# A chunked RWKV-7 mixer: 128x128 block-diagonal matrices kept as two 64x64 blocks, each product issued as two on opposite quarters of TensorE

## What is computed

```python
def rwkv7_scan(r, w, k, v, a, bvec):
    decay = jnp.exp(-jnp.exp(w))
    def step(state, inp):
        r_t, d_t, k_t, v_t, a_t, b_t = inp
        sa = jnp.einsum('bhvk,bhk->bhv', state, a_t)
        state = (state * d_t[:, :, None, :] + sa[..., None] * b_t[:, :, None, :]
                 + v_t[..., None] * k_t[:, :, None, :])
        return state, jnp.einsum('bhvk,bhk->bhv', state, r_t)
    ...
# in rwkv7_mixer, with kk normalised per head:
y = rwkv7_scan(rh, heads(w), kh, vh, -kk, kk * ah)
```

## Time and profile before

| | |
|---|---|
| median of 3 runs | 3529.41 us |
| the profiled execution | 3524.7 us, its span 3522.9 us |
| PE busy | 3341.1 us (95%) |
| DVE busy | 1490.8 us (42%) |
| ACT busy | 1082.6 us (31%) |
| POOL busy | 395.9 us (11%) |
| matmul records | 16568 |

### The profile page before, as it was taken

The page is one execution under the profiler, slowest core; times in us unless marked ns, Lnnn a source line. Parts: engine busy times, 40 slices in busy tenths (PEclk is TensorE's granted clock), DMA queues, the critical chain, the costliest instruction groups (busy, mean ns, idle before and its releaser), DMA issues. The chain is left out here.

```text
span 3522.9 us, 38396 instructions
## 1 busy us (share of the span) xinstructions
PE 3341.1 (95%) x16568; PEld 2582.1 (73%) x16568; DVE 1490.8 (42%) x2056; ACT 1082.6 (31%) x1619; POOL 395.9 (11%) x386
## 2 busy tenths in 40 slices
PE   6999999889899999999999989999998999999999
PEld 2466666666758888888877766788886888888887
DVE  6256624665444111113346442556543433333333
ACT  4243324334233111112135553233323322222211
POOL 1022202343212000000012000111211100000000
PEclk9999999999999999999999999899998999999999
DMA  5111110000042111112122010000003111110211
GB/s 234 41 60 61 72 39 24 13 13 24 1 153 75 48 48 48 48 36 91 46 72 83 36 37 18 8 1 1 1 1 150 54 48 48 48 48 30 96 44 71
DMA packets 35257, 182.33 MB, mean 52 GB/s; under 512 B 4261, under 2 KB 4261, under 8 KB 21648
## 3 DMA queue, kind: packets, MB, share of 16 engines
q1 hardware_dynamic: 22176, 133.18, 10.6%
q0 software_dynamic: 12912, 46.69, 3.4%
HBM read 161.89 MB, written 17.96 MB: 51 GB/s over the span
## 5 line engine op out<-in xcount | busy, mean ns | idle before, releaser
L537 PE MATMUL ps<-r,r 128*128 128x512 f32 x2656 | 1056.7, 398 | 14.4 <-DVE r L2022 13.2
L538 PE MATMUL ps<-r,r 128*128 128x512 f32 x2656 | 1048.0, 395 | 0.0
L539 PE MATMUL ps<-r,r 128*128 128x512 f32 x2656 | 1047.9, 395 | 0.0
L537 PEld LDWEIGHTS ps<-r,r 128*128 128x128 f32 x2656 | 501.4, 189 | 142.1 <-issue 20.7
L538 PEld LDWEIGHTS ps<-r,r 128*128 128x128 f32 x2656 | 501.7, 189 | 117.2 <-issue 3.0
L539 PEld LDWEIGHTS ps<-r,r 128*128 128x128 f32 x2656 | 501.4, 189 | 115.7
L1407 ACT ACTIVATE ar<-ps 128x512 f32<-128x512 f32 (+3 forms) x330 | 170.1, 541 | 628.1 <-PE ps L1214 119.5
L1369 ACT ACTIVATE r<-ar 128x1024 fp32r<-128x1024 f32 (+1 forms) x170 | 174.4, 1032 | 550.6 <-PE ps L539 510.6
L2015 DVE TENSOR_TENSOR r<-ar,r 128x1024 fp32r<-128x1024 f32 (+1 forms) x170 | 203.8, 1199 | 324.1 <-ACT r L1369 324.0
L527 PE MATMUL ps<-ar 128*128 128x128 f32 (+5 forms) x1844 | 278.0, 314 | 6.4 <-ACT ar L1407 3.3
L527 PEld LDWEIGHTS ps<-ar 128*128 128x128 f32 (+2 forms) x1844 | 218.9, 174 | 57.1 <-issue 31.8
(11 more groups left out here) (286 smaller groups left out, 3561.4 us busy)
## 6 DMA issues: line engine op xcount, KB each, us to landing
ar<-in_w_mod SPq DMA_DIRECT2D x24, 1024.0 KB, 4.8
ar<-in_w_gu SPq DMA_DIRECT2D x22, 1024.0 KB, 4.8
ar<-in_w_up SPq DMA_DIRECT2D x22, 1024.0 KB, 4.8
ar<-in_w_in SPq DMA_DIRECT2D x19, 1024.0 KB, 4.8
ar<-in_w_dn SPq DMA_DIRECT2D x32, 512.0 KB, 3.4
x<-ar POOLq DMA_DIRECT2D x48, 256.0 KB, 2.3
ar<-x POOLq DMA_DIRECT2D x24, 512.0 KB, 7.0
ar<-in_xT POOLq DMA_DIRECT2D x16, 512.0 KB, 13.7
```

Of the source, the lines that this page charges most:

```text
L537: M.matmul(o, whk, hi[k][:, a:a + n], start=k == 0, stop=False)
L538: M.matmul(o, whk, lo_[k][:, a:a + n], start=False, stop=False)
L539: ins = M.matmul(o, wlk, hi[k][:, a:a + n], start=False, stop=k == nk - 1)
```

## The change

The two diagonal blocks of a 128x128 matrix are kept one above the other: block 0 in partitions 0 to 63, block 1 in partitions 64 to 127, both in the same 64 columns. Four matrices now take 256 columns instead of 512. Each of the 4 matmuls of an `outer`, a `quad`, `pp` or `uw` becomes two of 64x64, one for each block h: it reads the rows of block h and writes the partitions of block h. In a `quad`, `pp` and `uw` the two lie on opposite quarters of the array (rows and output partitions both 0-63, or both 64-127). In an `outer` both read the same 64 rows (the head's channels) and write different halves of the partitions.

DVE, ACT and POOL work on 128x256 where they worked on 128x512. `rb` and `rk` are still needed as full 128x128 matrices (for `ru` and `ry`): `spread` writes their blocks to their places, as two instructions of 64x256 each instead of one of 128x512, and POOL sets the rest of the four buffers to zero once, ahead of the first mask. The masks shrink to ten of 64 columns.

```diff
+    rmask = r8.tile(10 * 64)
...
+    HALF = (slice(0, 64), slice(64, 128))
...
-    temps = [halves[j] + [r8.tile(256)] for j in range(2)]
+    temps = [[x[:, 0:256] for x in halves[j]] + [r8.tile(256)] for j in range(2)]
...
+                QUARTERS = [(n_, h) for n_ in range(4) for h in range(2)]
...
                 def outer(what, x, y):
                     key = (what, g_)
                     o = claim(key, next_of(BG), (v_evac, key))
-                    for n_ in range(4):
-                        ins = M.matmul(o[:, n_ * 128:n_ * 128 + 128], x[R, cs_(n_)], y[R, cs_(n_)], start=True, stop=True)
+                    for n_, h in QUARTERS:
+                        c = n_ * 128 + 64 * h
+                        ins = M.matmul(o[HALF[h], c64(n_)], x[R, c:c + 64], y[R, c:c + 64], start=True, stop=True)
...
                 def quad(key, x, y, *by):
-                    for n_ in range(4):
-                        ins = M.matmul(o[:, n_ * 128:n_ * 128 + 128], x[:, cs_(n_)], y[:, cs_(n_)], start=True, stop=True)
+                    for n_, h in QUARTERS:
+                        ins = M.matmul(o[HALF[h], c64(n_)], x[HALF[h], c64(n_)], y[HALF[h], c64(n_)],
+                                       start=True, stop=True)
...
-                for n_ in range(4):
-                    ins = M.matmul(o[:, n_ * 64:n_ * 64 + 64], AK[:, cs_(n_)],
-                                   Vt[:, n_ * 128 + 64 * j:n_ * 128 + 64 * j + 64], start=True, stop=True)
+                for n_, h in QUARTERS:
+                    ins = M.matmul(o[HALF[h], c64(n_)], AK[HALF[h], c64(n_)],
+                                   Vt[HALF[h], n_ * 128 + 64 * j:n_ * 128 + 64 * j + 64], start=True, stop=True)
...
+                    for Hh in HALF:
+                        M.matmul(o[Hh, n_ * 128:n_ * 128 + 64], TT_[Hh, c64(n_)],
+                                 At[Hh, n_ * 128 + 64 * j:n_ * 128 + 64 * j + 64], start=True, stop=True)
+                    for Hh in HALF:
+                        ins = M.matmul(o[Hh, n_ * 128 + 64:n_ * 128 + 128], TT_[Hh, c64(n_)],
+                                       PP[Hh, c64(n_)], start=True, stop=True)
...
-                        copy(("tnn", g_, Lv), TN, bank(("tnn", g_, Lv)))
-                    copy(("tt", g_, Lv), TT_, bank(("tt", g_, Lv)))
+                        copy(("tnn", g_, Lv), TN, bank(("tnn", g_, Lv), 256))
+                    copy(("tt", g_, Lv), TT_, bank(("tt", g_, Lv), 256))
...
-                    V.tensor_tensor(th(dst), th(bank(key)), bc4(m), ALU.mult).then_inc(*v_evac(key))
+                    V.tensor_tensor(th(dst, 64), th(bank(key, 256), 64), bc4(m, w_=64), ALU.mult).then_inc(*v_evac(key))
+
+                def spread(what, dst):
+
+                    key = (what, g_)
+                    dve.wait_ge(*product.at(key))
+                    for h, Hh in enumerate(HALF):
+                        ins = V.tensor_tensor(th(dst[Hh, :])[:, :, 64 * h:64 * h + 64], th(bank(key, 256)[Hh, :], 64),
+                                              bc4(M_IU, Hh, w_=64), ALU.mult)
+                    ins.then_inc(*v_evac(key))
...
+        for i in range(2):
+            G.memset(Arbs[i], 0.0)
+            G.memset(Arks[i], 0.0).then_inc(*p_mask(("zero", i)))
```

More of the change, by code:

```diff
@@ L418, in emit @@
     r8 = Region(H, FT)
-    rmask = r8.tile(9 * 128)
-    M_SU, M_IU, M_LO = [rmask[:, j * 128:j * 128 + 128] for j in range(3)]
-    M_UP = {1 << j: rmask[:, (3 + j) * 128:(4 + j) * 128] for j in range(6)}
+    rmask = r8.tile(10 * 64)
+    M_SU, M_IU, M_LO = [rmask[:, j * 64:j * 64 + 64] for j in range(3)]
+    M_UP = {1 << j: rmask[:, (3 + j) * 64:(4 + j) * 64] for j in range(6)}
+    M_ID = rmask[:, 576:640]
+    HALF = (slice(0, 64), slice(64, 128))
     MTs, NNs, SSs = [[r.tile(512) for r in (r8, r9)] for _ in range(3)]
@@ L1199, in group, with c64 @@
                 a0 = j * 512
-                def cs_(b_):
-                    return slice(b_ * 128, b_ * 128 + 128)
+                QUARTERS = [(n_, h) for n_ in range(4) for h in range(2)]
+                def c64(n_):
+                    return slice(n_ * 64, n_ * 64 + 64)
                 def outer(what, x, y):
@@ L2709, in group @@
                 dve.wait_ge(*v_evac.last())
-                V.tensor_tensor(th(TN), th(TN), bc4(IDN), ALU.add).then_inc(*v_step())
-                V.tensor_tensor(th(TT_), th(AT), bc4(M_UP[1]), ALU.mult).then_inc(*v_step())
+                V.tensor_tensor(th(TN, 64), th(TN, 64), bc4(M_ID, w_=64), ALU.add).then_inc(*v_step())
+                V.tensor_tensor(th(TT_, 64), th(AT, 64), bc4(M_UP[1], w_=64), ALU.mult).then_inc(*v_step())
                 dve.wait_ge(*v_step.last())
-                V.tensor_tensor(th(TT_), th(TT_), bc4(IDN), ALU.add).then_inc(*v_step(("tn", g_)))
+                V.tensor_tensor(th(TT_, 64), th(TT_, 64), bc4(M_ID, w_=64), ALU.add).then_inc(*v_step(("tn", g_)))
                 yield
                 masked("ak", AK, M_SU)
-                masked("rb", Arb[:, a0:a0 + 512], M_IU)
+                if s < 2:
+                    dve.wait_ge(*p_mask.at(("zero", s)))
+                spread("rb", Arb[:, a0:a0 + 512])
                 yield
-                masked("rk", Ark[:, a0:a0 + 512], M_IU)
+                spread("rk", Ark[:, a0:a0 + 512])
                 yield
@@ L2722, in group @@
                     dve.wait_ge(*product.at(key))
-                    V.tensor_tensor(th(Yp), th(bank(key)), bc4(IDN), ALU.add).then_inc(*v_evac(key))
+                    V.tensor_tensor(th(Yp, 64), th(bank(key, 256), 64), bc4(M_ID, w_=64), ALU.add).then_inc(*v_evac(key))
                     yield
@@ L2939, in gpsimd_program @@
                         pool.wait_ge(*product.at(("y", (s, j), Lv // 2)))
-                    G.tensor_tensor(th(AM), th(AT), bc4(M_UP[Lv]), ALU.mult).then_inc(*p_mask(("am", (s, j), Lv)))
+                    G.tensor_tensor(th(AM, 64), th(AT, 64), bc4(M_UP[Lv], w_=64),
+                                    ALU.mult).then_inc(*p_mask(("am", (s, j), Lv)))
         stage_over(pool, "rwkv", 0)
@@ L3109, in layout @@
           for L in (1, 2, 4, 8, 16, 32)]
-    m["rmask"] = np.concatenate(rm + [up[0].T] + up, 1).astype(f)
+    rm = [np.concatenate([x[:64, :64], x[64:, 64:]], 0) for x in rm + [up[0].T] + up + [i[:, None] == i[None]]]
+    m["rmask"] = np.concatenate(rm, 1).astype(f)
     m["rst64"] = np.tile((r(1024) % 64 != 0).astype(f), (128, 1))
```

## The result

The changed kernel takes 3431.32 us (median of 4 runs, 3430.62 to 3432.82) against 3529.42 us: a ratio of 0.9728, 95% interval 0.9714 to 0.9743, 98 us less. I had forecast 3472, with 3428 to 3522 as the range: the direction and the range held, the likeliest case did not. What came lies nearest my fourth rival, "the clock holds", with 16 us more than its 82. The result is only 3 us inside the lower end of the range.

What follows compares the result with a forecast made beforehand. TensorE was taken to bound the mixer, with DVE as much the bound in rounds 0 to 2. 82 us gained less 25 for the clock gave 57 off 3524.7, 3467.7, plus 4.7 for the median: 3472 us, range 3428 to 3522.

Steps and rivals of the forecast that it cites:

- fourth rival: Whole mixer: the clock does not fall, so the 82 us gain stands, 3430 to 3450 us; chance 0.18.
- price of a quad: TensorE's quads: 0.92 us before, 0.47 after if opposite quarters overlap, 0.93 as the other end if not.
- second rival: TensorE's quads: opposite quarters do not keep the pace, a quad costs up to 0.93 us, 3517 to 3535 us; chance 0.06.
- The five stretches: A full mixer step at full clock, priced in five parts: -14.0 us of 69.2 in sum.
- Rounds 0 to 2: Outer products until the first `y`, bound by DVE: narrower DVE operations give -2.5 us, 12.7 to 10.2.
- Levels 2 to 8: 18 quads save 8.1 us, new waits behind `prepare` and `finish` charged +2.0: 21.3 to 15.2 us.
- Levels 16 and 32: 12 quads save 5.4 us, waits for ACT's copies and `finish` charged +2.6: 14.1 to 11.3 us.
- What the clock gives back: Clock falls more often and returns later: 9 us of each step at half clock, 25 us lost in all.
- the case that I feared: First rival: TensorE's clock stays at 1.2 GHz through the mixer's steps, 3583 to 3691 us; chance 0.11.
- Step 0: First mixer step, without `finish` and starting at half clock: taken as -12 us.
- Steps 2 to 5: Later mixer steps, priced like step 1 at -14.0 us each; steps 1 to 5 together -70 us.
- the third: Rounds 0 to 8: DVE becomes the bound, 4 us a step of the gain lost, 3496 to 3520 us; chance 0.10.

Runs made afterwards that it cites:

- run 1: Changed kernel with both block products of each quad pair sent to block 0's quarter, DVE's `y` and ACT's level copies covering 64 partitions: 3644.28 us, ratio 1.0333.
- run 3: Changed kernel with only the outer products run block by block, four products then four, quads still in opposite pairs: 3430.89 us, ratio 0.9728.
- Run 5: Changed kernel with DVE taking the operations of `finish` ahead of those of `prepare` in each round: 3433.35 us, ratio 0.9736.
- run 7: Changed kernel with `mt`, `nn`, `ru` and `ry` of the two groups all interleaved on opposite quarters: 3419.16 us, ratio 0.9693.
- runs 6 and 10: Changed kernel with `mt` and `nn` of the two groups interleaved on opposite quarters: 3426.28 us; the same plus `ry` in pairs, `ru` not: 3399.03 us.

## Why the prediction was right in direction and 41 us too careful

The 41 us are the 25 that I took off for the clock and 16 more that the sum of the stretches missed.

- **The price of a quad: right.** 0.47 taken, 0.50 measured, and the other end, 0.93, is what one quarter costs in run 1. The rule of the Trainium skill, "TensorEngine Tiling (Array Packing)", section "Instruction Overhead" (some 60 cycles for each matmul), did not bring the second rival, and I had worked it out wrongly: 60 cycles at 2.4 GHz are 0.025 us, so 16 records would be 0.40 us (an estimate from the page's figure), below 0.47 and not near 0.93. The measured 0.031 us is 74 cycles a record, so the figure is not refuted, and by the rule splitting these products further would gain little. No run here tried that.
- **Widths: right.** DVE 0.42 and ACT 0.38 as priced; POOL's mask 0.80, in its bounds and hidden.
- **The five stretches: right in sum, by errors that cancel.** Forecast -14.0 for step 1, measured 69.21 to 55.07, -14.1. That is luck in part.
  - Rounds 0 to 2: -2.5 forecast, -3.3 measured. My items (-1.6, +0.6, -1.6 to -2.5) add up to -2.6 to -3.5, so the -2.5 was a slip.
  - Levels 2 to 8: -6.1 against -5.5. PE's idle time rose by 1.5 us (1.60 to 3.11), where I had charged 2.0, and 1.9 us of a fall of the clock that I had booked elsewhere is in it.
  - `ry`: 0 against +0.3, the rest of that fall.
  - Levels 16 and 32: -2.8 against -3.5, by a miscount and a wrong charge. They hold 10 quads, not 12 (records rise from 99 to 182, 8 for each quad). In the timelines the ten fall from 9.0 to 5.4 us, the wide products between them take 0.6 us more, and PE's wait, which I had charged with +2.6, fell from 1.74 to 1.20 us.
  - `pp` to `ru`: -2.6 against -2.2.
- **"What the clock gives back": this is the step that failed.** I charged 25 us, for 9 us more of each step at half clock, and nothing like that came. Falls did come where there had been none: one each in steps 1 and 4 and a second one in step 0. Steps 2 and 3 have one in both kernels. In step 1 it begins 1.3 us behind the 1.74 us wait:

```profile
2316.20:2319.60 3.40, 3.40 (x47) 2.83 (x41) 0.70 (x2) 1.57 (x6) 0.00 (x0) 0.50 0.02 5
```

  It is 3.4 us long and not 9, about 1.5 us lost at my 0.45 (an estimate), and it is already in the measured stretches. Nor is a long wait a sure sign. In step 4 the fall begins at 2469.9, 0.7 us behind a wait of 0.70 us, and the clock stays at 1.00 behind this one:

```profile
2481.18 2.08 PE L1221 MATMUL ps<-ar 64*64 64x64 f32 x64 [2.07 <-DVE ar L2744]
```

  So which waits bring a fall is not shown. The second half of the reasoning, that pairs of quarters bring the clock back later than full quads, did not come true: the fall of step 2 lasts 3.4 us before and 3.4 us now. Over the six steps the time at half clock went from 40.9 us (23.9, 3.4, 3.4, 10.2) to 37.5 (13.7, five of 3.4, 6.8) instead of growing by 54. Run 1 shows the case that I feared, with quads on one quarter.
- **Step 0: too small, 7 of the 16 us.** -12 forecast, -18.7 measured. It starts at half clock, and that time itself shrank from 23.9 us to 13.7:

```profile
2244.50:2258.20 13.70, 13.70 (x176) 8.95 (x173) 8.47 (x20) 4.96 (x7) 2.07 (x3) 0.50 0.01 3
2258.20:2271.80 13.60, 9.53 (x257) 8.16 (x255) 11.87 (x23) 5.65 (x13) 4.75 (x6) 1.00 0.01 2
```

  The clock is back 0.9 us after the first quad (2257.31), but the pairs of the quads are not the reason: in run 1, with quads on one quarter, it is back 0.9 us after the first of them too (2249.63, 2250.50). It is the outer products that matter here. With these in turn and the quads in pairs (run 3) it comes back 4.1 us after the first quad, and the step is 3.6 us longer. I had seen no gain in cheaper outers.
- **Steps 2 to 5: too small, the rest of the 16 us.** Steps 2 and 3, with a fall of the clock in both kernels, saved 15.9 and 15.8 us, which is what a step saves when the clock does the same; step 4, with a new fall, saved 14.9, all against 14. Step 5 has no `prepare`, and there DVE hardly holds TensorE up: its levels 2 to 8 (2599.63 to 2620.37 before, 2521.52 to 2532.91 now) fell by 9.4 us, where I had 6.1 with a charge of 2.0 for waits behind `prepare`. I had priced it like the others; it saved 19.2.
- **The rivals.** The second is refuted by the pace, the third by DVE's durations; DVE does bound rounds 0 to 2 (9.13 busy of 9.45), and most of the waits of `st` are for its update of the state. Run 5 shows that its order is not the cure.

## What to carry to other kernels

Two small products that drive opposite quarters of the array, issued in turn, cost little more than one of them; look for twins (two groups, two blocks) even where each product is already as small as it can be, and begin with those that nothing else has to keep up with, as `ry` here. After each such saving look for the longest new wait of TensorE and at what runs behind it: behind waits of 2.1 to 2.3 us ahead of `ru` and the outer products the clock fell for 17 us in three steps of run 7, though not in every step, and the kernel was 20 us slower than with `ru` left alone; behind the 0.8 us waits of runs 6 and 10 it did not. Price the clock by what follows the fall, not by the fall.

## What the runs showed that I had not expected

- A busy TensorE can stay at 1.2 GHz: 75.1 us on end with PE busy 73.9 us, with all its quads on one quarter (run 1). In step 0 of the same run such quads ran at 2.4 GHz for 16.8 us, until the clock fell.
- Outer products on one group's 64 rows, alternating between output halves, run at 0.029 us a record at the full clock: in the changed kernel's timeline 64 of them start 1.84 us before the next product. But in step 0 and in run 7 the clock stayed at 1.2 GHz during such products. How they are ordered counts: step 0's first stretch at half clock is 13.7 us with the two halves of the partitions in turn product by product, on whichever quarters the quads then run (the changed kernel and run 1), and 20.3 us with four products of one half and then four of the other (run 3).

```profile
2292.86 1.91 PE L1215 MATMUL ps<-ar 64*64 64x64 f32 x64
2294.70 1.13 PE L1160 MATMUL ps<-ar 32*128 32x512 f32 x4
```

- Taking the pairs apart, four products by four, costs 0.008 us a record (0.031 to 0.039), not the whole overlap.
